# Turning two 32 by 32 grids on VectorE in place of 64 TensorE transposes, with the scores one chunk sooner and one low part on GpSimd

## The reference, cut to what matters

```python
h = xn @ w_in                                   # 2048 x 8192: q, k, v, gate
s = einsum("bqhcd,bkhcd->bhcqk", q, k) + bias   # 8 heads, two score maps each
p = softmax(s)
a = p[:, :, 0] - lam * p[:, :, 1]
o = einsum("bhqk,bkhe->bqhe", a, v)             # head width 256
o = o * rsqrt(mean(o * o) + eps) * head_gain * (1 - lambda_init)
x = x + (o * silu(gate)) @ w_out
```

## Time and profile before

| | us |
|---|---|
| median of 3 runs (lowest, highest) | 861.33 (860.55, 861.74) |
| the profiled execution, its time | 861.68 |
| the profiled execution, its span | 859.9 |
| TensorE busy | 851.1 |
| VectorE busy | 594.8 |
| ScalarE busy | 447.9 |
| GpSimd busy | 215.6 |

### The profile page before, as it was taken

How to read it: one execution, slowest core, us unless ns; L and a number is a source line. 1 busy time by engine, 2 the same in 40 slices (tenths; PEclk the granted TensorE clock), 3 DMA queues, 4 the chain that set the end, 5 groups by cost and what they waited for, 6 DMA issues and landing times.

```text
span 859.9 us, 13887 instructions
## 1 busy us (share of the span) xinstructions
PE 851.1 (99%) x5694; PEld 778.3 (91%) x5694; DVE 594.8 (69%) x966; ACT 447.9 (52%) x586; POOL 215.6 (25%) x74
## 2 busy tenths in 40 slices
PE   9999999999999999999999999999999999999996
PEld 8988899889988899888888899999999999998885
DVE  6567554684457454685588977999999998566651
ACT  7756543546336543567444455455554555694432
POOL 0000000000000000000000007888888878680000
PEclk9999999999999999999999999999999999999999
DMA  9976565555554565543556655565556555549502
GB/s 327 394 279 236 165 211 185 192 166 171 179 186 146 165 214 183 191 147 121 175 194 196 195 195 162 184 197 184 178 180 196 176 173 193 186 158 342 185 11 99
DMA packets 99089, 163.75 MB, mean 190 GB/s; under 512 B 3504, under 2 KB 39600, under 8 KB 98520
## 3 DMA queue, kind: packets, MB, share of 16 engines
q1 hardware_dynamic: 97408, 160.50, 55.6%
q10 hardware_dynamic: 1624, 2.45, 0.8%
HBM read 160.83 MB, written 3.69 MB: 191 GB/s over the span
## 4 chain that ended last, share of the span: by engine, by line
PE 95%; DVE 2%; DMA 1%; SPq 1%; ACT 0%; issue 0%
PE ps_acc L1212 17%; PE ps_acc L1215 17%; PE ps_acc L1214 17%; PE ps_acc L1201 13%; PE ps_acc L1198 13%; PE ps_acc L1200 13%; DMA sb_w_raw<-in_attn_w_in 1%; PE ps_a L1162 1%; DVE sb_w_lo L784 1%; PE ps_a L1312 0%; PE ps_a L1311 0%; SPq L325 0%; PE ps_a L1310 0%; PE ps_d L1289 0%; PE ps_d L1288 0%; PE ps_d L1287 0%
## 5 line engine op out<-in xcount | busy, mean ns | idle before, releaser
L432 ACT ACTIVATE sb_w_hi<-sb_w_raw 128x2048 fp32r<-128x2048 f32 x140 | 267.6, 1916 | 268.8 <-PE ps_acc L1215 173.4
L784 DVE TENSOR_TENSOR sb_w_lo<-sb_w_raw,sb_w_hi 128x2048 fp32r<-128x2048 f32 x96 | 219.3, 2291 | 144.1 <-ACT sb_w_hi L432 143.8
L1212 PE MATMUL ps_acc<-sb_conv_hi,sb_w_hi 128*128 128x256 f32 x768 | 215.4, 280 | 0.0
L1215 PE MATMUL ps_acc<-sb_conv_hi,sb_w_lo 128*128 128x256 f32 x768 | 214.3, 279 | 0.0
L423 POOL TENSOR_TENSOR sb_w_lo<-sb_w_raw,sb_w_hi 128x2048 fp32r<-128x2048 f32 x44 | 203.9, 4640 | 41.2 <-ACT sb_w_hi L432 41.2
L1214 PE MATMUL ps_acc<-sb_conv_lo,sb_w_hi 128*128 128x256 f32 x768 | 214.2, 279 | 0.0
L1003 DVE SCALAR_TENSOR_TENSOR ps_d<-sb_uT,sb_dwT,ps_d 128x256 f32<-128x256 f32 x480 | 188.9, 487 | 4.5 <-ACT ps_d L666 4.5
L1198 PE MATMUL ps_acc<-sb_w_hi,sb_act_hi 128*128 128x512 f32 x384 | 152.2, 396 | 0.0
L1201 PE MATMUL ps_acc<-sb_w_hi,sb_act_lo 128*128 128x512 f32 x384 | 151.6, 395 | 0.0
L1200 PE MATMUL ps_acc<-sb_w_lo,sb_act_hi 128*128 128x512 f32 x384 | 151.6, 395 | 0.0
L1214 PEld LDWEIGHTS ps_acc<-sb_conv_lo,sb_w_hi 128*128 128x128 f32 x768 | 144.1, 188 | 0.1
(11 more groups left out here) (171 smaller groups left out, 872.3 us busy)
## 6 DMA issues: line engine op xcount, KB each, us to landing
sb_w_raw<-in_attn_w_in SPq DMA_DIRECT2D x60, 1024.0 KB, 5.6
sb_w_raw<-in_conv_w_in SPq DMA_DIRECT2D x64, 512.0 KB, 4.6
sb_w_raw<-in_attn_w_out SPq DMA_DIRECT2D x16, 1024.0 KB, 5.0
sb_w_raw<-in_conv_w_in SPq DMA_DIRECT2D x16, 1024.0 KB, 5.1
sb_w_raw<-in_conv_w_out SPq DMA_DIRECT2D x16, 1024.0 KB, 5.0
sb_w_raw<-in_attn_w_in SPq DMA_DIRECT2D x4, 512.0 KB, 8.6
sb_xs<-in_x SPq DMA_DIRECT2D x2, 1024.0 KB, 15.5
sb_w_raw<-in_attn_w_in SPq DMA_DIRECT2D x7, 256.0 KB, 4.5
```

The source lines that it names most:

```text
L432: act.activation(w_hi[slot][:], w_raw[slot][:], ACT.Copy).then_inc(hi_ready, 1)
L784: dve.tensor_tensor(w_lo[slot][:], w_raw[slot][:], w_hi[slot][:].bitcast(F32), ALU.subtract).then_inc(lo_ready, 1)
L1212: pe.matmul(into, left_hi, hi[:, kt], start=(kt == 0 and f % 2 == 0), stop=False, skip_group_check=True)
L1215: ins = pe.matmul(into, left_lo, hi[:, kt], start=False, stop=(kt == KT - 1), skip_group_check=True)
```

## The change

The probabilities are no longer turned on TensorE. In slot 12 VectorE turns them with sixteen STREAM_TRANSPOSE instructions from `probs[:, :, 0]` into `probs[:, :, 1]`; ScalarE and VectorE make their high and low parts from there. The scores, their maxima and exponentials move one slot forward (slots 9 and 10), and the joining of the softmaxes moves from slot 12 to slot 11, ahead of v's low part. The gated output is written back into `o_rows` and turned by VectorE, sixteen instructions behind the low part of slot 15 of each pair, into a tile `mT` with features on the partitions, which replaces `m_rows`; the splits for the output projection (`m_high`, `m_low`) read `mT`. The low part of chunk 67, which VectorE would make in slot 15 of the last pair, is made by GpSimd. VectorE's loop over the middle pairs is unrolled.

```diff
+POOL_SEAM = CHUNKS_ATT + RING - 1
-                m_rows = sb("m_rows", [P, ST, D], F32, two)
+                mT = sb("mT", [P, KT, SEQ], F32, two)
+                probs_turned = probs[:, :, 1].rearrange("p a (k r) -> p a k r", k=ST)
+        def by_pool(c):
+            return c == POOL_SEAM or POOL_FROM <= c < POOL_TO
+        def by_query_tile(part, h):
+            return part[:, h].rearrange("p k (q r) -> p q k r", q=ST)
# GpSimd
+            low_part(POOL_SEAM)
# ScalarE
-                if i in (10, 11):
+                if i in (9, 10):
                     high_part(16 * j + i + RING, i % NCH, 4 * j + i // NCH + 2)
-                    for hq in ((0, 1) if i == 10 else (2, 3)):
+                    for hq in ((0, 1) if i == 9 else (2, 3)):
...
                 if i == 13:
+                    act.wait_ge(probs_turned_done, j + 1)
                     for h in range(2):
-                        high_of_a(A + h, h, a_parts[0][:, h].rearrange("p k s -> p (k s)"))
+                        act.activation(by_query_tile(a_parts[0], h), probs_turned[:, 2 * h:2 * h + 2], ACT.Copy
+                                       ).then_inc(a_hi_ready, 1)
...
+            def m_high(n):
+                act.wait_ge(m_turned, 1 + n + 1)
+                act.wait_ge(w_free, RING + CHUNKS_ATT - NCH + n + 1)
+                for kt in range(4 * n, 4 * n + 4):
+                    act.activation(act_hi[:, kt], mT[:, kt], ACT.Copy, scale=vecs[:, G_HEAD, kt:kt + 1]
+                                   ).then_inc(split_hi, 1)
# VectorE
+                if i == 12:
+                    dve.wait_ge(a_ready, 4 * (j + 1))
+                    for a in range(P // Q):
+                        for b in range(P // Q):
+                            src = probs[a * Q:(a + 1) * Q, :, 0].rearrange("p h (k b c) -> p b h k c", b=P // Q, c=Q)
+                            ins = dve.transpose(probs_turned[b * Q:(b + 1) * Q, :, :, a * Q:(a + 1) * Q], src[:, b])
+                    ins.then_inc(probs_turned_done, 1)
+                    for h in range(2):
+                        dve.wait_ge(a_hi_ready, 2 * j + h + 1)
+                        dve.tensor_tensor(by_query_tile(a_parts[1], h), probs_turned[:, 2 * h:2 * h + 2],
+                                          by_query_tile(a_parts[0], h).bitcast(F32), ALU.subtract
+                                          ).then_inc(a_lo_ready, 1)
...
-                low_part(16 * j + i + RING, i % NCH)
+                if not by_pool(16 * j + i + RING):
+                    low_part(16 * j + i + RING, i % NCH)
+                if i == 15:
+                    dve.wait_ge(m_ready, 4 * (j + 1))
+                    if j == PAIRS - 1:
+                        dve.wait_ge(k_ready, 2 * PAIRS)
+                    for a in range(P // Q):
+                        for b in range(P // Q):
+                            src = o_rows[a * Q:(a + 1) * Q].rearrange("p s (f b c) -> p b s f c", b=P // Q, c=Q)[:, b]
+                            dst = mT[b * Q:(b + 1) * Q, 4 * j:4 * j + 4].rearrange(
+                                "p f (s a r) -> p a s f r", s=ST, a=P // Q)[:, a]
+                            ins = dve.transpose(dst, src)
+                    ins.then_inc(m_turned, 1)
...
+            def m_low(n):
+                dve.wait_ge(m_turned, 1 + n + 1)
+                for kt in range(4 * n, 4 * n + 4):
+                    dve.wait_ge(split_hi, KT + kt + 1)
+                    dve.scalar_tensor_tensor(act_lo[:, kt], mT[:, kt], vecs[:, G_HEAD, kt:kt + 1],
+                                             act_hi[:, kt].bitcast(F32), ALU.mult, ALU.subtract).then_inc(m_split, 1)
-            with dve.Fori(1, PAIRS - 1) as j:
+            for j in range(1, PAIRS - 1):
# TensorE
-                if i in (10, 11):
+                if i in (9, 10):
...
-                if i == 13:
-                    pe.wait_ge(a_ready, 4 * (j + 1))
-                    for h in range(2):
-                        free_a(A + h)
-                        for kt in range(ST):
-                            for qt in range(ST):
-                                ins = turn(bank_a[h][:, kt * SEQ + qt * P:kt * SEQ + (qt + 1) * P],
-                                           probs[:, 2 * h + qt, 0, kt * P:(kt + 1) * P])
-                        ins.then_inc(a_full, 1)
                 if i == 14:
                     pe.wait_ge(acc_free, 4 + 2 * (4 * j + 3))
-                    pe.wait_ge(a_free, 2 + A + 2)
+                    pe.wait_ge(a_lo_ready, 2 * (j + 1))
+                    pe.wait_ge(a_free, 2 + A)
...
-                if 12 <= i < 15:
-                    m_fills(i - 12)
...
-                    pe.wait_ge(d_free, 2 + D_M + 2 * (i + 1))
-                pe.wait_ge(lo_ready, c + 1)
+                    pe.wait_ge(m_split, CK * (i + 1))
+                low_part_ready(pe, c)
-                if i == 0:
-                    m_fills(3)
```

More of the change, by code:

```diff
@@ L291, in piece_landed @@
             return landed[slot] if closes else head_landed[pieces_left_open(p)]
+        def by_pool(c):
+            return c == POOL_SEAM or POOL_FROM <= c < POOL_TO
         def low_part_ready(eng, c):
[L295 to L300, removed]
+            done = sum(by_pool(b) == by_pool(c) for b in range(c + 1))
+            eng.wait_ge(lo_ready_pool if by_pool(c) else lo_ready, done)
         def scaled_by(g):
             return 4 + 2 * (G_CONV_IN + g + 1)
+        def by_query_tile(part, h):
+            return part[:, h].rearrange("p k (q r) -> p q k r", q=ST)
         def gated_bank(b):
@@ L867, in pair_slot @@
                         dve.tensor_tensor(lo, k_scaled[:, f], hi.bitcast(F32), ALU.subtract).then_inc(acc_free, 1)
[L868 to L872 removed]
+                if i in (9, 10):
+                    if i == 9:
                         dve.wait_ge(bias_landed, 16 * (j + 1))
                         dve.wait_ge(a_full, A_START + A_PER_PAIR * j)
[L875 removed]
+                    for hq in ((0, 1) if i == 9 else (2, 3)):
                         h, qt = hq // 2, hq % 2
@@ L909, in pair_slot @@
                                                  ALU.mult, ALU.add).then_inc(a_ready, 1)
+                    for st in range(ST):
+                        dve.wait_ge(part_hi, 2 * j + st + 1)
+                        dve.scalar_tensor_tensor(v_parts[1][:, st], acc[:, st], rstd[:, st:st + 1],
+                                                 v_parts[0][:, st].bitcast(F32), ALU.mult, ALU.subtract
+                                                 ).then_inc(acc_free, 1)
+                if i == 12:
[10 more added lines that the diff above has]
+                                          ).then_inc(a_lo_ready, 1)
                 if i == 14:
@@ L968, in _ @@
                 if i == 0:
[L969 removed]
+                    m_low(3)
                 if i % NCH == NCH - 1:
@@ L1177, in sums_and_line @@
                 pe.matmul(bank_a[1][0:HEADS, :], table[:], hot[:], start=True, stop=True).then_inc(a_full, 1)
-            def fill_features(n, rows, f):
-                free_d(n)
-                for e in range(2):
-                    for st in range(ST):
-                        kt = 2 * f + e
-                        ins = turn(bank_d[n % 2][:, e * SEQ + st * P:e * SEQ + (st + 1) * P],
-                                   rows[:, st, kt * P:(kt + 1) * P])
-                ins.then_inc(d_full, 1)
             def project(i, par, hi, lo, halfway=None, tiles=range(ST), done=w_free, filled=False):
@@ L1276, in pair_slot @@
                         project(i % NCH, t % 2, act_hi, act_lo)
-                if i in (10, 11):
-                    if i == 10:
+                if i in (9, 10):
+                    if i == 9:
                         pe.wait_ge(acc_free, 4 + 2 * (4 * j + 2))
-                    for hq in ((0, 1) if i == 10 else (2, 3)):
+                    for hq in ((0, 1) if i == 9 else (2, 3)):
                         h, qt = hq // 2, hq % 2
```

90 lines of the change are left out of this document (24 added, 66 removed).

## The result

The changed kernel takes **851.9 us** (median of 5 runs, 851.78 to 852.14) against 861.33 us in 5 runs beside it: ratio 0.9892 [0.9882, 0.9903]. The forecast was 854.1 us with a range of 853.4 to 856.6. The profiled execution took 852.14 us with a span of 850.4 (before: 861.68 and 859.9), so the trace has 9.5 us to explain.

The account below looks back on a forecast made before the run. TensorE's queue, busy 99% of the span, was taken as the bound. Eight blocks (6.93 us) plus a 0.33 us wait gave 7.26 off 861.68, 854.4; less 0.35 for the median, 854.1 us, range 853.4 to 856.6.

Parts of the forecast that it names:

- What bounds the kernel: Whole kernel: TensorE, busy 99% of the span, sets the time; an edit gains what it takes out of its queue.
- Eight blocks at 0.87 and a wait of 0.33, 7.26 us: TensorE, four pairs: removing eight transpose blocks saves 6.93 us, and the fourth pair's bank wait 0.33 us; together 7.26.
- VectorE's 14.3 us a pair, and the ring: VectorE takes on 14.3 us per pair, to 68.8 of 95.8; the ring of weight chunks survives, slack 6 us.
- The chain to the output matmuls: Third pair: A's parts ready at 287.7, TensorE at 288.9; slack 1.2 us, 1.0 in the first pair.
- The strided copies: Copies from VectorE's turned probabilities, not in the trace; at twice 0.616 us each they end just in time.
- Without the earlier scores, 4.4 us of waiting four times: Chain to the output matmuls, 5.6 us longer without earlier scores: 4.4 us waits in four pairs, exceeding the whole gain.
- The seam: Fourth pair's end: gated output split by 409.6, TensorE wants it at chunk 67, 410.9; slack 1.3 us.
- Rival (a): Seam: GpSimd and VectorE hold each other off, TensorE waits 3.3 us once, time 857.4; chance 0.09.
- (b): Chain to the output matmuls exceeds its slack by 0.4 to 0.6 us: four waits, about 856.3; chance 0.08.
- (c): VectorE's turn sets the end: unseen strides slow its transposes; at 0.75 us each, 872 us; chance 0.06.
- (d): TensorE's waits for low parts take back what the blocks gave (x near 2.7): 861 us; chance 0.03.
- Nothing else changes: Stages behind 410 us: no other change, so they simply move 7.3 us forward.

Follow-up runs that it names:

- gated_only: Kernel before with only the gated output turned on VectorE and chunk 67's low part on GpSimd; probabilities and scores as before: 857.49 us, ratio 0.9956.
- probs_only: Kernel before with only the probabilities turned on VectorE and the scores one chunk earlier; TensorE still turns the gated output: 866.7 us, ratio 1.0059.
- chain_plus_two: Changed kernel with two more VectorE transposes in each pair, ahead of the sixteen of the probabilities: 851.66 us, ratio 0.9891.
- chain_plus_five: Changed kernel with five more VectorE transposes in each pair, ahead of the sixteen of the probabilities: 855.27 us, ratio 0.9932.
- seam_on_vector: Changed kernel with the low part of chunk 67 back on VectorE, ahead of the last turn: 853.21 us, ratio 0.9905.
- after: The changed kernel itself, against the kernel before: 851.9 us, ratio 0.9892; measured again unaltered, 852.0 us.
- seven_nudges: Changed kernel with seven extra 128-column float32 matmuls in the convolution stage, behind chunks 5, 13, 17, 22, 26, 31 and 35: 850.81 us, ratio 0.988.
- ten_nudges: seven_nudges with three more such matmuls, one behind slot 15 of each of the first three pairs: 851.91 us, ratio 0.9892.
- before_nudged: Kernel before with one extra 128-column float32 matmul behind chunk 5 of the convolution stage: 859.58 us, ratio 0.998.
- break_kinds: Changed kernel with 29 extra breaks of five kinds (transposes or float32 matmuls, results unused) in the convolution stage: 863.15 us, one run.
- scores_late: Changed kernel with the scores back behind chunks 10 and 11 and the softmax join behind them in slot 11: 872.08 us, ratio 1.0121.

## Why the prediction was right, and where it was wrong

- *What bounds the kernel:* right. TensorE stays at 99%, and the time moved with its queue.
- *Eight blocks at 0.87 and a wait of 0.33, 7.26 us:* right, 7.4 measured between the head and the convolution stage, and 3.8 for the half of it in gated_only. The other half is not worth its 3.5 us on its own, though, which the prediction did not ask: probs_only is 5.4 us slower than before. The forecast of 7.26 held since both went together.
- *VectorE's 14.3 us a pair, and the ring:* right. The windows show 67.9 us for 68.8 forecast, and no low part is late.
- *The chain to the output matmuls:* right to the tenth. Slack 1.2 us in the third pair and 1.0 in the first, and chain_plus_two and chain_plus_five bracket it from both sides. The strided copies, bounded at twice their price, took 0.62 and 0.69 us each, no more than the copies of the earlier trace rows.
- *Without the earlier scores, 4.4 us of waiting four times:* right in kind. It was 3.4, since the late order takes a low part out of the chain, and the time rose by 5.0 for each on average, more than the whole gain, as said. What the sum lacked is the clock, which that kernel's trace shows at 0.50 behind the wait.
- *The seam:* right, 1.0 us of slack for 1.3. seam_on_vector, forecast at 0.9 us of waiting, waits 1.1.
- *Rival (a), GpSimd and VectorE hold each other off:* empty. Transposes of 7.19 us beside GpSimd's low part and 7.18 without it. The Trainium skill, SBUF — State Buffer, section "Who interferes with whom", whose rule is that a VectorE instruction with at most one SBUF input, outside the two-port modes, doesn't collide with GpSimd, agrees with this.
- *Rivals (b), (c), (d):* empty. A transpose of the probabilities takes 0.448 us. chain_plus_five shows that their mechanism is real, some 0.9 us a pair once the chain is 1.87 longer. The rule of the Trainium skill that was weighed (VectorE: DVE Perf Modes, "Rules for kernel authors": a 128x128 transpose goes to TensorE where PSUM can take it) is not borne out here: TensorE was the full engine, and the move off it paid, by 7.4 us. No run here has VectorE full, so none shows where the rule would hold.
- *"Nothing else changes", and that the stages behind 410 us simply move 7.3 us forward:* **this is the step that failed.** The convolution stage has the same matmuls in the same order without a wait, and the part of it in the account above is 273.11 us long in place of 275.02. The sum had no term for it. I had taken the step of an unchanged matmul as fixed, and the trace of before held rows against that: its own last five chunks behind the `spread` step at 113.3 ns. A range whose lower end stood 0.7 us below the forecast had no room for 1.9 us of this. The other 0.2 us lie in the first 50 us of the program, where traces of the same instructions differ by up to 1.5 us (after, seven_nudges, ten_nudges).

With these terms, all read from the two traces afterwards, the sum is 861.68 - 7.4 - 1.9 - 0.2 = 852.2, against 852.14 in the profiled run. That the prediction got the direction and most of the size is by its mechanism; that 1.9 us came on top was luck.

Shown: the extra 1.9 us lie in the step of 432 matmuls, came again in the second trace of the same kernel, and don't belong to the turn on VectorE (before_nudged has them, gated_only doesn't). Open: what at a break decides between the two steps. It is not the clock (1.00 in both), nor the DMA share (0.57 in both), nor the kind of break alone, nor TensorE's order of matmuls alone (seam_on_vector has the order of the changed kernel and other quick stretches; the start of break_kinds is quick where the same instructions aren't elsewhere). That it depends on the state in which TensorE comes to the break would fit the runs, but no run measured such a state.

## What to carry to other kernels

Read the difference of the starts of the same matmul stage by stage, also where "nothing changes": of a gain of one per cent on a kernel that TensorE bounds, a fifth was here the luck of a step that an unrelated matmul also gives, so a change should be judged on the stage that it touches. A chain added up row by row on the clock of the kernel before came out to a few tenths of a microsecond here (slack 1.2 for 1.2, and 1.0 for 1.3), and moving its source one chunk sooner made the slow turn free. Ask of each half of a change what it does without the other: the half that fills an engine's queue may stand on the half that takes a hand-over out of it.

## What the runs showed of the hardware that I had not expected

- Matmuls of 128x256 with their own weights step by 117.8 or by 113.3 ns, at the same granted clock; the value changes only where the stream is broken, by other instructions or (break_kinds, 29.7 us) by a short pause. One 128-column float32 matmul in the right place made the kernel before 1.7 us faster, and seven in the wrong place made the kernel after 4.2 us slower.
- A wait of TensorE of 3.4 us cost 4.9 to 6.3 us in the trace of scores_late, since the granted clock is 0.50 for 2.9 to 6.1 us of work behind it. Waits of 1.1 us (seam_on_vector) and of 0.6 to 0.8 us (chain_plus_five) left it at 1.00.
- Two and five extra transposes in a row added 0.68 and 1.87 us, 0.34 and 0.37 each, less than the 0.448 of the sixteen; why is open.
